# Second layer's sample rows: queries spread over partitions by one-hot products, heads copied a bank at a time

## What is computed

```python
def dilated_sample(q, buf, kv_new, window, dil):
    comb = jnp.concatenate([buf, kv_new], axis=1)
    idx = lb + jnp.arange(t)[:, None] - jnp.arange(steps + 1)[None, :] * dil
    valid = idx >= 0
    sel = jnp.take(comb, jnp.maximum(idx, 0), axis=1)
    o, lse = local_attend(q[:, :, None], sel[:, :, :, 0], sel[:, :, :, 1], valid[:, None, :])

def combine_groups(outs, lses):
    w = jax.nn.softmax(jnp.stack(lses), axis=0).astype(outs[0].dtype)
    return jnp.einsum('gbth,gbthe->bthe', w, jnp.stack(outs))
```

## Time and profile before

| | us |
|---|---|
| median of 3 runs | 1663.02 |
| lowest and highest of them | 1662.4, 1663.4 |
| the profiled execution | 1667.32 |
| its span in the trace | 1665.5 |
| block of the change in the span | from 1246.7 to 1339.1 |

### The profile page before, as it was taken

One profiled execution on the slowest core, in us unless ns is written; L12 is line 12 of the kernel. 1 busy time (PEld: TensorE's weight loads), 2 busy tenths in 40 slices (PEclk: granted clock), 3 DMA queues, 4 the chain that ended last, 5 costly groups with the idle time before them and its releaser, 6 DMA issues. The chain is left out here.

```text
span 1665.5 us, 20629 instructions
## 1 busy us (share of the span) xinstructions
PE 1397.0 (84%) x8266; PEld 969.1 (58%) x8266; DVE 602.0 (36%) x856; ACT 371.2 (22%) x669; POOL 477.6 (29%) x522
## 2 busy tenths in 40 slices
PE   5899999986699988848999999999973668998882
PEld 4677777543566645436768678587461255665451
DVE  1355552413311111143355446535245642111113
ACT  3243443311112211120023032141040111221110
POOL 3233325300001101025683765645500001111000
PEclk9999999998599999959999999999995558999996
DMA  7834423401799999672121111120107177999994
GB/s 263 310 115 132 134 77 115 179 1 54 320 360 420 420 420 421 259 228 56 34 72 48 45 46 41 52 73 13 33 9 212 42 299 304 421 420 421 420 384 166
DMA packets 149513, 326.31 MB, mean 196 GB/s; under 512 B 57880, under 2 KB 103416, under 8 KB 124736
## 3 DMA queue, kind: packets, MB, share of 16 engines
q1 hardware_dynamic: 134432, 287.21, 46.2%
q0 software_dynamic: 13824, 33.84, 5.6%
q10 hardware_dynamic: 1184, 4.26, 0.7%
HBM read 307.48 MB, written 34.29 MB: 205 GB/s over the span
## 5 line engine op out<-in xcount | busy, mean ns | idle before, releaser
L1574 PE MATMUL ps<-wB,xT_b 128*128 128x384 f32 x768 | 265.1, 500 | 3.3 <-DVE wB L1810 3.3
L943 PE MATMUL ps<-wg,oT 128*64 128x256 f32 x1024 | 236.0, 384 | 20.0 <-DMA wd<-in_w_down 18.4
L943 PE MATMUL ps<-wu,oT 128*64 128x256 f32 x1024 | 236.3, 384 | 0.0
L1574 PEld LDWEIGHTS ps<-wB,xT_b 128*128 128x128 f32 x768 | 204.8, 272 | 48.7 <-issue 5.5
L943 PEld LDWEIGHTS ps<-wg,oT 128*64 128x64 f32 x1024 | 139.2, 138 | 75.3 <-DMA wd<-in_w_down 27.3
L467 PE MATMUL ps<-xnT_a,wA 128*128 128x260 f32 (+1 forms) x768 | 171.0, 382 | 2.8 <-DMA wA<-in_w_qkv_a 1.6
L943 PEld LDWEIGHTS ps<-wu,oT 128*64 128x64 f32 x1024 | 139.2, 138 | 36.7 <-issue 16.6
L467 PEld LDWEIGHTS ps<-xnT_a,wA 128*128 128x128 f32 x768 | 144.6, 190 | 26.7 <-issue 4.1
L1334 POOL DMA_INDIRECT y_rows<-ysb,idx x32 | 32.1, 1003 | 435.3 <-DVE ysb L978 435.3
L961 PE MATMUL ps<-wd,hT 128*64 128x512 f32 x512 | 124.0, 601 | 30.4 <-DVE hT L972 30.4
L969 DVE TENSOR_TENSOR h<-sg,ps 64x256 f32<-64x256 f32 x64 | 26.4, 413 | 236.9 <-ACT sg L966 227.4
(11 more groups left out here) (258 smaller groups left out, 2136.0 us busy)
## 6 DMA issues: line engine op xcount, KB each, us to landing
wg<-in_w_gate SPq DMA_DIRECT2D x64, 1024.0 KB
wu<-in_w_up SPq DMA_DIRECT2D x64, 1024.0 KB
wd<-in_w_down SPq DMA_DIRECT2D x64, 1024.0 KB
wA<-in_w_qkv_a SPq DMA_DIRECT2D x24, 512.0 KB, 5.9
wB<-in_w_q_b SPq DMA_DIRECT2D x12, 1024.0 KB, 7.5
wB<-in_w_kv_b SPq DMA_DIRECT2D x24, 256.0 KB, 4.0
work<-in_w_qkv_a SPq DMA_DIRECT2D x1, 4096.0 KB
vres<-qa_rows SPq DMA_DIRECT2D x8, 512.0 KB, 5.2
```

The source lines that it names most:

```text
L943: last = nc.tensor.matmul(bank(q)[lo:lo + CAP, 0:FE], x[:, k, :], wt[:, k, :], start=(k == 0), stop=(k == KT - 1))
L1574: last = nc.tensor.matmul(bank(c % 2)[:, 0:UW], xT[:, kt, cols], wB[:, g, kt, :], start=(kt == 0), stop=(kt == KT - 1))
```

## The change

- The constants get 16 more blocks of 128 columns: `sel`, 24 partitions by 16 units by 128. Column m of block u is one-hot: its 1 stands at the row of the query that partition m of unit u needs. They stand behind the old constants in device memory, and the load of the old constants reads the first 2253 columns.
- `qb` and its 32 broadcasts are gone. In their place are `qsrc` (24 partitions by 1024, all queries, 96 KB) and `sel` (192 KB), one transfer each, ahead of the first keys.
- TensorE makes the queries of unit u in banks 2 (u % 2) and the next one: two products of 512 columns, `sel` block u as the weights, `qsrc` moving. It does so one after the other, and after every second unit one `out_b.product`, which all stood at the start of the block before. Unit u waits until VectorE has done product u - 2 (`s_e`), whose banks it takes over.
- VectorE's product reads the queries from the two banks, and waits for the keys and for `s_q`.
- The heads are copied a bank at a time, all 128 partitions, two copies for eight. `oh_b` isn't zeroed any more.

```diff
+                    sp.dma_start(qsrc[:, :], q_rows.rearrange("g b j e -> (g b) (j e)")).then_inc(s_qin, 16)
+                    sp.dma_start(sel[:, :, :], a["const"][0:NDIL * DEC, NCONST:].rearrange("p (u m) -> p u m", m=128)).then_inc(s_qin, 16)
                     for b in range(DEC):
-                        queries(0, b, 128, 0, 0)
                         sp.dma_start(kb[:, b, 0, :], a["cache_kv_b1"][b].rearrange("s c h e -> s (c h e)")).then_inc(s_kb[b][0], 16)
...
-                        for g, lo, hi in ranges:
-                            queries(g, b, hi - lo, 1, lo)
                         sp.dma_start(kb[0:n1 - 1, b, 1, :], a["cache_kv_b2"][b, 0:PAST:4].rearrange("s c h e -> s (c h e)")).then_inc(s_kb[b][1], 16)
...
                 def _(pe):
-                    for i in range(8):
-                        out_b.product(pe, 1, i)
+                    pe.wait_ge(s_qin, 32)
+                    for u in range(NSEL):
+                        if u >= 2:
+                            pe.wait_ge(s_e, u - 1)
+                        rows = S1ROWS if u % 2 else 128
+                        for n in range(2):
+                            last = nc.tensor.matmul(bank(2 * (u % 2) + n)[0:rows, :], sel[:, u, 0:rows], qsrc[:, 512 * n:512 * n + 512],
+                                                    start=True, stop=True)
+                        last.then_inc(s_q, 1)
+                        if u % 2:
+                            out_b.product(pe, 1, u // 2)
...
-                        dve.wait_ge(s_kb[b][tile], 16 * (5 if tile else 2))
+                        dve.wait_ge(s_kb[b][tile], 32 if tile else 16)
+                        dve.wait_ge(s_q, u + 1)
...
-                                        qb[0:rows, tile, b, :].rearrange("p (j i e) -> p j i e", j=NKV, i=4), ALU.mult).then_inc(s_e, 1)
+                                        bank(2 * tile, 2)[0:rows, :].rearrange("p (j i e) -> p j i e", j=NKV, i=4), ALU.mult).then_inc(s_e, 1)
...
-                        for i in range(4):
-                            rows = slice(32 * i, 32 * i + NH)
-                            V.tensor_copy(oh_b[rows, q, :], bank(q)[rows, 0:NKV * HD]).then_inc(s_ohc, 1)
+                        V.tensor_copy(oh_b[:, q, :], bank(q)[:, 0:NKV * HD]).then_inc(s_ohc, 1)
```

More of the change, by code:

```diff
@@ L50 @@
 S1ROWS = PAST // 4 + 1 + PAST // 16 + 1 + 1
+NSEL = 2 * DEC
 def constants():
-    c = np.zeros((128, NCONST), np.float32)
+    c = np.zeros((128, NCONST + NSEL * 128), np.float32)
     def put(name, a):
@@ L95, in constants @@
     put("sel8", (p % 32) - (32 - DEC) == np.arange(DEC)[None, :])
+    n1, n2 = PAST // 4 + 1, PAST // 16 + 1
+    group = np.stack([np.zeros(128), np.where(np.arange(128) < n1, 1, np.where(np.arange(128) < n1 + n2, 2, 0))])
+    row_of = group[None, :, :] * DEC + np.arange(DEC)[:, None, None]
+    c[:, NCONST:] = (p == row_of.reshape(1, -1)).astype(np.float32)
     put("eps", np.full(128, EPS))
@@ L284, in _ @@
                     if t == 0:
-                        sp.dma_start(cst[:, :], a["const"]).then_inc(s_const, 16)
+                        sp.dma_start(cst[:, :], a["const"][:, 0:NCONST]).then_inc(s_const, 16)
                 norm.load(sp)
@@ L2010, in layer_b @@
                 kb = sb("kb", [128, DEC, 2, 512], to=ph)
-                qb = sb("qb", [128, 2, DEC, D], to=ph)
+                qsrc = sb("qsrc", [NDIL * DEC, D], to=ph)
+                sel = sb("sel", [NDIL * DEC, NSEL, 128], to=ph)
                 oh_b = sb("oh_b", [128, 2, NKV * HD], to=ph)
-                s_oh0, s_ohc, s_ot = (sem("bs_" + n) for n in ("heads_zeroed", "heads_copied", "heads_turned"))
+                s_ohc, s_ot = (sem("bs_" + n) for n in ("heads_copied", "heads_turned"))
+                s_qin, s_q = sem("bs_queries_in"), sem("bs_query_rows")
                 s_op, s_od, s_oa, s_os = (sem("bs_" + n) for n in ("parts_done", "parts_copied_dve", "parts_copied_act", "parts_summed"))
@@ L2031, in _ @@
                     next_norm.load(sp)
-                    def queries(g, b, rows, tile, lo):
-                        q = q_rows[g, b].partition_broadcast(rows)
-                        sp.dma_start(qb[lo:lo + rows, tile, b, :].rearrange("p (j e) -> p j e", j=NKV), q).then_inc(s_kb[b][tile], 16)
+                    sp.dma_start(qsrc[:, :], q_rows.rearrange("g b j e -> (g b) (j e)")).then_inc(s_qin, 16)
+                    sp.dma_start(sel[:, :, :], a["const"][0:NDIL * DEC, NCONST:].rearrange("p (u m) -> p u m", m=128)).then_inc(s_qin, 16)
                     for b in range(DEC):
-                        queries(0, b, 128, 0, 0)
                         sp.dma_start(kb[:, b, 0, :], a["cache_kv_b1"][b].rearrange("s c h e -> s (c h e)")).then_inc(s_kb[b][0], 16)
@@ L2070, in _ @@
                     for q in range(2):
-                        pe.wait_ge(s_ohc, 4 * q + 4)
+                        pe.wait_ge(s_ohc, q + 1)
                         for j in range(NKV):
@@ L2096, in _ @@
                     V = nc.vector
-                    V.memset(flat(oh_b), 0.0).then_inc(s_oh0, 1)
                     V.memset(SS[:, 1, :, :], NEG).then_inc(s_z, 1)
@@ L2124, in _ @@
                     V.tensor_copy(pt[:, :, :].rearrange("p a b -> p (a b)"), bank(5)[:, 0:256]).then_inc(s_pc, 1)
-                    dve.wait_ge(s_oh0, 1)
                     for q in range(2):
                         dve.wait_ge(s_pv, q + 1)
-                        for i in range(4):
-                            rows = slice(32 * i, 32 * i + NH)
-                            V.tensor_copy(oh_b[rows, q, :], bank(q)[rows, 0:NKV * HD]).then_inc(s_ohc, 1)
+                        V.tensor_copy(oh_b[:, q, :], bank(q)[:, 0:NKV * HD]).then_inc(s_ohc, 1)
                     dve.wait_ge(s_ot, 1)
```

## The result

The changed kernel is slower, not faster: 1678.29 us (1673.99 to 1681.98, 4 runs) against 1663.21 us for the kernel before in the same comparison. The ratio is 1.0071, with a 95% interval of 1.0048 to 1.0093. I had predicted 1648.7 us. The profiled execution of the changed kernel took 1673.99 us, with a span of 1672.0 us; it is the fastest of the four.

A forecast was written before the change was run, and what follows sets the result against it. Transfers in turn with VectorE were taken to bound the scores stretch. The walk's -13.1 and the head copies' -1.2 gave -14.3 us, from the median 1663.02 to 1648.7 us; own range 1643 to 1656, reaching on to 1659.

The forecast's parts named there:

- What bounds the kernel now: Scores stretch: VectorE's key-query product waits 22.4 us for transfers; without that a sequence takes 5.61 us.
- rival C: 24-row transfers go through one DMA engine, 11 us instead of 0.7; 1658.7 us; chance 0.05.
- Start: Block start: TensorE waits for qsrc and sel and starts at 1252.0, bounds 1251.3 and 1253.5.
- A unit on TensorE: Two products of 512 columns, four records: 3.44 us at half clock, 1.72 at full; weight rows cost nothing.
- The clock: TensorE in the scores stretch: full clock 5 us after its start, at 1257.0, and staying up.
- rival A: Clock stays at half, TensorE is the bound over 96 records; 1683.0 us, slower; chance 0.10.
- The walk: Unit by unit through the scores: VectorE bound at 5.61 us a sequence, last sum at 1300.2 for 1313.31, -13.1 us.
- Break-even: Scores stretch: gain used up where 96 records take 62.6 us, 0.65 us a record or 0.66 of full clock.
- rival B: Clock comes and goes, mean 0.8, 6.45 us a sequence; 1654.6 us, faster still; chance 0.06.
- VectorE's product from the banks: VectorE's product reading queries from PSUM: 1225 ns for 1221 from SBUF, 0.1 us over sixteen, taken as zero.
- Head copies: Behind the scores: two copies for eight let TensorE start on the first bank, -1.2 us, bounds -1.0 and -1.8.
- Tail's clock: Turns, value products, sample projection: taken unchanged; up to 5 us go if clock holds, up to 2 come if later.

The follow-up runs named there:

- even_rows: Kernel before, with its broadcasts over 65 and 17 partitions each cut into 64 or 16 plus a single one, nothing else: 1650.2 us, ratio 0.9902.
- rows128: Changed kernel with one-hot products widened from 24 to 128 weight rows, added weights zero, added moving rows other numbers: 1655.3 us, ratio 0.9941.
- rowtiles: Changed kernel with a sequence's four one-hot products side by side on TensorE, from four partition groups: 1651.8 us, ratio 0.9923.
- early_warm: rowtiles with an earlier block start, plus three spare 128-row products at each of two TensorE waits behind the scores: 1643.1 us, ratio 0.9861.
- proj_last: Changed kernel with all eight projection units behind the sixteen one-hot units instead of between them: 1674.0 us, ratio 1.0044.
- dense24: Changed kernel with 24 weight rows of dense random numbers in place of the one-hot ones: 1678.4 us, ratio 1.0078.
- zeros128: As rows128, but the moving operand's added rows are zeros too: 1656.6 us, ratio 0.9935.

## Why the prediction was wrong, step by step

- **What bounds the kernel now: right.** VectorE waited for transfers whose rows don't divide well; even_rows takes 15 us of its 22.4 us of waiting away by recutting them. "Two of the broadcasts with odd counts are slow" in rival C goes further than the rows: they point at the 17-row ones only. I saw the one engine at 26 GB/s, and didn't ask whether the transfers could simply be cut otherwise.
- **Start: mis-sized.** TensorE started 6.2 us after the block's start, not 5.3, and VectorE's first product came 10.15 us after it (1243.05 to 1253.20) instead of 8.95. That is 1.2 us. Rival C is out: the 24-row transfers did not take 11 us.
- **A unit on TensorE: right at a given clock.** A record at half clock has the 0.86 us that I took from the projection (54.98 us for 64), and the rows cost nothing by themselves. The Trainium skill, "TensorE: Matmul & The Clock Gate", section "Why this matters for your kernels", says of a contraction over 32 rows too that a single product takes as long as one over 128, and the trace agrees for the single record.
- **The clock: the step that failed.** I took the clock to rise 5 us after the start and to stay up because TensorE would be busy. Busy it was, 73.72 of 74 us, and the mean was 0.59. The Trainium skill, "TensorE: Matmul & The Clock Gate", Part 1, ties full clock to sustained busy time in its table of states; by these rows that isn't enough: 54 us without a gap brought no rise with 24 weight rows, and 128 rows, even of zeros, held 1.00. I had the missing piece as rival A, with a chance of 0.10. What argued against it there, "the one-hot ones have the same 512 columns", was about columns when the question was rows; the row of narrow products at 0.50 had shown that "busy" alone doesn't decide.
- **The walk: right under its condition, wrong in the sum.** In rows128 and rowtiles a sequence takes 5.61 us, as put. In the changed kernel the seven steps from the first product of sequence 0 to that of sequence 7 (1315.79) took 62.6 us for 39.6. These 23 us are nearly the whole miss in the trace: with the late start, 1.2, and 1.0 us of waiting inside the last sequence, they turn -13.1 into +12.0 us at the last sum. The medians miss by 29.4 us (+15.1 for -14.3), 3.9 more than the block in the two traces (+11.2), and no trace shows where those 3.9 lie.
- **Break-even: not contradicted.** I had put the gain used up at 0.66 of full clock. The changed kernel had 0.59 and lost, which is a single point; its times (1674.0 to 1682.0) lie between rival B's 1654.6 and rival A's 1683.0.
- **VectorE's product from the banks: right.** 1219 ns in the median for 1220 before. The Trainium skill, "VectorE: DVE Perf Modes", section "The TRN2 errata", has 62 cycles more for a PSUM source, by my estimate 65 ns; they don't show.
- **Head copies: right,** 1.3 us in the trace for 1.2.
- **Tail's clock: as put** for the changed kernel (25.2 us for 26.0, of which the copies are more than all). early_warm, whose tail takes 19.6 us with the same copies, shows that the 5 us that I kept as a bound are there to be had.

## What to carry to other kernels

Before replacing a transfer by products on TensorE, work out TensorE's time at half clock, and count on full clock only if a trace shows it for products of that shape: here those with 128 weight rows had it and those with 24 did not. Small contractions should go side by side in groups of 32 partitions; in rowtiles that brought a sequence on TensorE down to about VectorE's time even at half clock. Before removing a slow broadcast, look at its row count: cutting one row off those over 65 and 17 partitions gave the whole gain here. A short chain of small products behind a wait can be worth some spare full-size products that fit into the wait (3.8 us here).

## What the runs showed of the hardware that I had not expected

- With 24 weight rows TensorE stayed at 0.50 through 54 us without a gap (proj_last), and dense numbers in them helped no more than one-hot ones (mean clock 0.57 and 0.59, dense24 and the changed kernel); with 128 rows of which 104 were zeros it had 1.00 over 40 us (zeros128).
- In the changed kernel the granted clock fell while TensorE worked without a gap: 1.00 in 1260 to 1262, 0.50 in 1264 to 1268, with 4.00 of 4.00 us busy.
- In early_warm, with the spare products just ahead, the granted clock stayed at 1.00 through 3.2 us of products with 16 or 64 weight columns (1298.29 to 1301.45). In proj_last, where TensorE had stood idle for 2.75 us a little earlier, it fell from 1.00 to 0.50 within the value products, between 1331 and 1332.
- Broadcasts over 65 and 17 partitions cost far more than the same rows as 64 + 1 and 16 + 1: the whole kernel is 1.0% faster with the eight of each cut so.

Left open is what the clock does between 24 and 128 weight rows, why half of the projection units in the changed kernel raised the clock and half did not, and why three of its four runs had less clock than the profiled one; no run here was made for any of them.
